# RWKV decay and a projections as three fp32r products on 64 rows each, masked scores in two buffers

## The reference, cut to what matters

```
r, rk, rv, wl, al = split(mixed, (512, 512, 512, 64, 64))     # mixed: (T, ...) after the token shift
w     = -softplus(-(w0 + tanh(wl) @ w_up)) - 0.5              # w_up: 64 x 512
decay = exp(-exp(w))
a     = sigmoid(a0 + al @ a_up)                               # a_up: 64 x 512
...                                                           # kk, rk, then the delta-rule scan
y     = rwkv7_scan(r, decay, rk, rv, kk, a)
```

## Time and profile before

| | |
|---|---|
| three runs | 3512.80, 3516.01, 3516.35 us, median 3516.01 |
| profiled execution | span 3515.1 us from its first to its last instruction; no time of its own is listed beside the span |
| PE | 3295.0 us busy, 94% of the span |
| DVE, ACT, POOL | 62%, 42%, 16% |
| granted TensorE clock, mean | 0.971 |
| the 32 projection matmuls, L274 | 64 records, from 40.2 to 817.4 us |

### The profile page before, as it was taken

The page is one execution under the profiler, slowest core; times in us unless marked ns, Lnnn a source line. Parts: engine busy times, 40 slices in busy tenths (PEclk is TensorE's granted clock), DMA queues, the critical chain, the costliest instruction groups (busy, mean ns, idle before and its releaser), DMA issues. The chain is left out here.

```text
span 3515.1 us, 75244 instructions
## 1 busy us (share of the span) xinstructions
PE 3295.0 (94%) x31246; PEld 2822.4 (80%) x31246; DVE 2186.4 (62%) x3701; ACT 1464.0 (42%) x2121; POOL 560.4 (16%) x792
## 2 busy tenths in 40 slices
PE   7999999999699998989979979949999999999997
PEld 5778888788577786867868868839999999999997
DVE  4666766667445655677777766666565655565563
ACT  5445444444255655332232223424444444444442
POOL 3455555554100000000000000000100110011000
PEclk9999999999899999989999999959999999999999
DMA  4221222211233434422121245436666666666662
GB/s 145 56 83 51 66 74 62 83 49 46 66 126 109 149 125 140 137 73 72 62 70 61 84 136 176 157 105 219 215 200 214 203 213 204 215 203 210 207 215 72
DMA packets 361838, 452.90 MB, mean 129 GB/s; under 512 B 15188, under 2 KB 300148, under 8 KB 361588
## 3 DMA queue, kind: packets, MB, share of 16 engines
q1 hardware_dynamic: 350200, 407.40, 35.7%
q0 software_dynamic: 9216, 33.56, 4.1%
q10 hardware_dynamic: 2176, 8.39, 0.6%
HBM read 382.17 MB, written 67.13 MB: 128 GB/s over the span
## 5 line engine op out<-in xcount | busy, mean ns | idle before, releaser
L2840 PE MATMUL bank<-ex_x_hi,ex_w_lo 128*128 128x256 f32 x2048 | 581.5, 284 | 2.0 <-DVE ex_x_lo L3022 2.0
L2841 PE MATMUL bank<-ex_x_lo,ex_w_hi 128*128 128x256 f32 x2048 | 580.2, 283 | 0.0
L2842 PE MATMUL bank<-ex_x_hi,ex_w_hi 128*128 128x256 f32 x2048 | 580.1, 283 | 0.0
L2836 DVE TENSOR_TENSOR ex_w_lo<-ex_w_loaded,ex_w_hi 128x2048 fp32r<-128x2048 f32 x192 | 433.9, 2289 | 226.7 <-ACT ex_w_hi L2832 222.3
L2832 ACT ACTIVATE ex_w_hi<-ex_w_loaded 128x2048 fp32r<-128x2048 f32 x192 | 359.4, 1904 | 172.5 <-PE bank L2842 169.3
L2840 PEld LDWEIGHTS bank<-ex_x_hi,ex_w_lo 128*128 128x128 f32 x2048 | 393.4, 192 | 2.8 <-issue 2.2
L2841 PEld LDWEIGHTS bank<-ex_x_lo,ex_w_hi 128*128 128x128 f32 x2048 | 393.5, 192 | 0.6
L2842 PEld LDWEIGHTS bank<-ex_x_hi,ex_w_hi 128*128 128x128 f32 x2048 | 393.5, 192 | 0.0
L2316 PE MATMUL bank<-sc_tokens_hi,sc_w_lo 128*128 128x512 f32 x672 | 267.7, 398 | 38.7 <-DVE hidden_hT_split L2428 16.0
L2896 POOL CAST ex_idx<-moe_idx_all 128x2 uint32 (+1 forms) x16 | 3.0, 186 | 1760.9 <-POOLq L79 1449.6
L2318 PE MATMUL bank<-sc_tokens_hi,sc_w_hi 128*128 128x512 f32 x672 | 265.0, 394 | 0.0
(11 more groups left out here) (485 smaller groups left out, 8312.5 us busy)
## 6 DMA issues: line engine op xcount, KB each, us to landing
ex_w_loaded<-in_wg SPq DMA_DIRECT2D x64, 1024.0 KB, 5.5
ex_w_loaded<-in_wu SPq DMA_DIRECT2D x64, 1024.0 KB, 6.5
ex_w_loaded<-in_wd SPq DMA_DIRECT2D x64, 1024.0 KB, 5.0
plain_weights<-in_w_in SPq DMA_DIRECT2D x70, 512.0 KB, 4.6
gl_ada_tile<-in_ada_w SPq DMA_DIRECT2D x48, 512.0 KB, 4.3
hidden_first_w<-in_sc_w_in SPq DMA_DIRECT2D x24, 1024.0 KB, 5.1
plain_columns<-hT_dram SPq DMA_DIRECT2D x14, 1024.0 KB, 7.4
plain_columns<-in_x SPq DMA_DIRECT2D x16, 512.0 KB, 5.7
```

Of the source, the lines that this page charges most:

```text
L2836: nc.vector.tensor_tensor(w_lo[c % SPLIT][:], raw[:, c % LOADED, :], w_hi[c % SPLIT][:].bitcast(F32), ALU.subtract).then_inc(s["lo"], 1)
L2840: nc.tensor.matmul(psum, ll, rh, start=first, stop=False)
L2841: nc.tensor.matmul(psum, lh, rl, start=False, stop=False)
L2842: return nc.tensor.matmul(psum, lh, rh, start=False, stop=last)
```

## The change

The projections become three fp32r products each, on the same 64 rows, in the order lo x hi, hi x lo, hi x hi, and in each of the three steps first the decay's matmul, then a's; both PSUM banks are taken ahead of the first. The operands `lup_hi`, `lup_lo` (once) and `lora_hi`, `lora_lo` (once a quarter) are made by ACT copies and DVE subtractions. The low parts lie where the plain `lup` and `lora` lay; the room for the high parts comes from the third `scm` buffer. PE now waits for `lora_lo`, and `low_lora` stands on DVE's list ahead of `mix_raw(i, "k", kx)`.

```
+        with Phase("rw_plain") as plain:
+            lup = sb(nc, plain, "lora_up", [P, HP, P])
+            lora = sb(nc, plain, "lora", [P, QT])
+        lup_lo = sb(nc, ctx, "lora_up_lo", [P, HP, P], F32R)
+        lora_lo = sb(nc, ctx, "lora_lo", [P, QT], F32R)
+        lup_hi = sb(nc, ctx, "lora_up_hi", [P, HP, P], F32R)
+        lora_hi = sb(nc, ctx, "lora_hi", [P, QT], F32R)
...
-        scm = [sb(nc, ctx, f"scores{i}", [P, 4, 4, 64]) for i in range(3)]
+        scm = [sb(nc, ctx, f"scores{i}", [P, 4, 4, 64]) for i in range(2)]
...
                 def decay_and_a(i):
-                    pe.wait_ge(s["lora"], i // HP + 1)
-                    for n in range(2):
-                        psum = begin(("wa"[n], i))
-                        nc.tensor.matmul(psum, lup[64 * n:64 * n + 64, i % HP, :], lora[64 * n:64 * n + 64, :], start=True, stop=True).then_inc(s["job"], 1)
+                    if i == 0:
+                        pe.wait_ge(s["up_lo"], 1)
+                    pe.wait_ge(s["lora_lo"], i // HP + 1)
+                    psums = [begin((name, i)) for name in "wa"]
+                    for m, (up, down) in enumerate(((lup_lo, lora_hi), (lup_hi, lora_lo), (lup_hi, lora_hi))):
+                        for rows, psum in zip(heads2, psums):
+                            mm = nc.tensor.matmul(psum, up[rows, i % HP, :], down[rows, :], start=(m == 0), stop=(m == 2))
+                            if m == 2:
+                                mm.then_inc(s["job"], 1)
...
                 def keep_lora(q):                                  # ACT
                     act.wait_ge(s["lmix"], q + 1)
-                    nc.scalar.activation(lora[0:64, :], lora[0:64, :], ACT.Tanh).then_inc(s["lora"], 1)
+                    nc.scalar.activation(lora_hi[64:128, :], lora[64:128, :], ACT.Copy)
+                    nc.scalar.activation(lora[0:64, :], lora[0:64, :], ACT.Tanh).then_inc(s["tanh"], 1)
+                    act.wait_ge(s["tanh"], q + 1)
+                    nc.scalar.activation(lora_hi[0:64, :], lora[0:64, :], ACT.Copy).then_inc(s["lora"], 1)
...
                 act.wait_ge(s["small"], 16 * SMALL)
+                nc.scalar.activation(lup_hi[:], lup[:], ACT.Copy).then_inc(s["up_hi"], 1)
...
+                def low_lora(q):                                   # DVE
+                    go.settle()
+                    dve.wait_ge(s["lora"], q + 1)
+                    nc.vector.tensor_tensor(lora_lo[:], lora[:], lora_hi[:].bitcast(F32), ALU.subtract).then_inc(s["lora_lo"], 1)
...
                         if (half, part) == (0, 2):
+                            low_lora(i // HP)
                             mix_raw(i, "k", kx)
...
+                dve.wait_ge(s["up_hi"], 1)
+                nc.vector.tensor_tensor(lup_lo[:], lup[:], lup_hi[:].bitcast(F32), ALU.subtract).then_inc(s["up_lo"], 1)
```

More of the change, by code:

```diff
@@ L117, in rwkv @@
             "hs0", "hs1", "hs2", "hs3", "w0", "w1", "w2", "w_hi", "w_lo", "job",
-            "lraw", "lmix", "lora", "tw", "sw", "ta", "cs", "pcs", "exps", "r_exp", "raw", "mixed", "kk", "kk_sq", "ssq",
+            "lraw", "lmix", "tanh", "lora", "lora_lo", "up_hi", "up_lo", "tw", "sw", "ta", "cs", "pcs", "exps", "r_exp", "raw", "mixed", "kk", "kk_sq", "ssq",
             "k_forms", "r_form", "rk", "n2_part", "n2", "tg", "gate", "bonus", "pre",
@@ L125, in rwkv @@
         wraw, w_lo, w_hi = [[whole[:, i * D:(i + 1) * D].rearrange("p (kb n) -> p kb n", n=P) for i in range(3)] for whole in (cols_buf.w, cols_buf.w_lo, cols_buf.w_hi)]
+        with Phase("rw_plain") as plain:
[5 more added lines that the diff above has]
+        lora_hi = sb(nc, ctx, "lora_hi", [P, QT], F32R)
         xst = sb(nc, ctx, "x_stat", [P, 4, 4])
         wc = sb(nc, ctx, "norm_cols", [P, KD])
-        lup = sb(nc, ctx, "lora_up", [P, HP, P])
         par = sb(nc, ctx, "head_params", [P, HP, 12])
@@ L133, in rwkv @@
         lraw = ob
-        lora = sb(nc, ctx, "lora", [P, QT])
         carry = sb(nc, ctx, "carry", [P, 2, HP, 3])
@@ L394, in inputs_of @@
                         for cr in heads2:
-                            mm = nc.tensor.matmul(bank[6][cr, p * C:p * C + C], scm[b % 3][cr, p, 2, :], tm[b % 3][cr, jj, 3, heads2[h]], start=True, stop=True)
+                            mm = nc.tensor.matmul(bank[6][cr, p * C:p * C + C], scm[b % 2][cr, p, 2, :], tm[b % 3][cr, jj, 3, heads2[h]], start=True, stop=True)
                     mm.then_inc(s["x"], 1)
@@ L415, in transfer @@
                             p, hs_, cr = 2 * h + jj, heads2[h], heads2[c]
-                            nc.tensor.matmul(bank[1 + c][hs_, 256 + jj * C:256 + jj * C + C], wun[cr, p, 0, :], scm[b % 3][cr, p, 1, :], start=True, stop=True)
+                            nc.tensor.matmul(bank[1 + c][hs_, 256 + jj * C:256 + jj * C + C], wun[cr, p, 0, :], scm[b % 2][cr, p, 1, :], start=True, stop=True)
                         for h, c in quads:
@@ L436, in y_inside @@
                         for cr in heads2:
-                            nc.tensor.matmul(bank[7][cr, o:o + C], scm[b % 3][cr, p, 3, :], tm[b % 3][cr, jj, 3, heads2[h]],
+                            nc.tensor.matmul(bank[7][cr, o:o + C], scm[b % 2][cr, p, 3, :], tm[b % 3][cr, jj, 3, heads2[h]],
                                              start=(p == 0), stop=False, skip_group_check=True)
                         for cr in heads2:
-                            mm = nc.tensor.matmul(bank[7][cr, o:o + C], scm[b % 3][cr, p, 1, :], wun[cr, p, 1, :],
+                            mm = nc.tensor.matmul(bank[7][cr, o:o + C], scm[b % 2][cr, p, 1, :], wun[cr, p, 1, :],
                                                   start=False, stop=False, skip_group_check=True)
@@ L1020, in keep_scores @@
                     for h in range(2):
-                        dst = scm[f % 3][:, 2 * h:2 * h + 2, :, :].rearrange("p j n t -> p j (n t)")
+                        dst = scm[f % 2][:, 2 * h:2 * h + 2, :, :].rearrange("p j n t -> p j (n t)")
                         nc.vector.tensor_tensor(dst, bank[1 + h].rearrange("p (j x) -> p j x", j=2), mk("scores").unsqueeze(1).to_broadcast([P, 2, 256]),
@@ L1159, in level_of @@
                     m = lm[:, l + 1, :].unsqueeze(1).to_broadcast([P, 2, C])
-                    nc.gpsimd.tensor_tensor(nt[:, l, 0:2, :], scm[g % 3][:, 0:2, 0, :], m, ALU.mult)
+                    nc.gpsimd.tensor_tensor(nt[:, l, 0:2, :], scm[g % 2][:, 0:2, 0, :], m, ALU.mult)
                     nc.gpsimd.tensor_tensor(nt[:, l, 2:4, :], across[:], m, ALU.mult).then_inc(s["nt"], 1)
@@ L1166, in corner @@
                     pool.wait_ge(s["n2"], i + 1)
-                    nil = scm[f % 3][:, :, 0, :]
+                    nil = scm[f % 2][:, :, 0, :]
                     by_head = nil.rearrange("p (h j) t -> p h j t", h=2)
@@ L1174, in corner @@
                     for c in range(2):
-                        ins = nc.gpsimd.tensor_copy(across[heads2[1 - c], :, :], scm[f % 3][heads2[c], 2:4, 0, :])
+                        ins = nc.gpsimd.tensor_copy(across[heads2[1 - c], :, :], scm[f % 2][heads2[c], 2:4, 0, :])
                     ins.then_inc(s["nil_across"], 1)
```

## The result

The changed kernel takes 3526.34 us (median of five runs, 3525.2 to 3535.2) against 3516.01 for the kernel before (3512.8 to 3518.31): ratio 1.0035, 95% interval 1.0025 to 1.0046. It is slower by 10.3 us, where no change was forecast; the time lies 0.34 us above the range. The profiled execution has a span of 3524.6 us and a mean granted clock of 0.971, as before.

The account below looks back on a forecast made before the run. PE, busy 94% of 3515.1 us, was taken to bound the kernel through its list. Terms of -2.1, +2.0 and 0 summed to -0.1 us, said as 3516.0 us, no change that can be told; range 3512.5 to 3526.

Parts of the forecast that it names:

- Side by side, 0.87 us: Projections on PE: both halves' fp32r matmuls overlap, three steps taking 0.87 us a tile against 1.06 for the plain ones.
- The twelve tiles: Tiles with `i % 4` not 0: 0.19 us less in eight, 0.14 in four held by DVE's L1043; 2.1 us less.
- Tiles 4, 8, 12, +0.68 each: `low_lora` ahead of `mix_raw(k)` delays `kx` and ACT's list behind it by 0.68 us each; 2.0 us more in all.
- Tile 0, start-up, score buffers, nothing: Added work hides behind existing waits in tile 0 and start-up; two score buffers bring no wait, no gain: 0 us.
- A: Projections: fp32r matmuls on different row halves run one after another; 9.6 us more, 3525.6 us; chance 0.19.
- B: Projections: each step pays its weight load, 0.32 us, so the twelve tiles gain about 0; +2.0, 3518 us; chance 0.05.
- D: Faster: the twelve tiles would have to gain 0.6 us each, which only new places in memory could do; chance 0.03.
- C: Clock falls to 1.2 GHz after PE's 1.9 us idle in tiles 4, 8, 12; 3 x 1.7 = +5.1, 3521 us; chance 0.05.

Follow-up runs that it names:

- the swapped order: The changed kernel with `mix_raw(k)` ahead of `low_lora` on DVE's list, PE's list as long as before: 3526.3 us, ratio 1.0028.
- the version without gaps: The changed kernel with 192 instructions of met waits added to PE's list, 128 at its head, 64 behind the first transposes: 3520.5 us, ratio 1.0012.
- the shift by 128: The changed kernel with 256 met waits, 128 instructions, at the head of PE's list: 3528.36 us, ratio 1.0045.

## Why the prediction was wrong

*Side by side, 0.87 us:* right. It measured 0.89 to 0.91, 0.16 less than the 1.06 of before instead of 0.19; in tiles 5, 9, 13 and 14 it is 1.02, 0.04 less instead of 0.14, and PE waits for L1063 there, as said. The 0.04 for 0.14 is a term of the sum that was mis-sized: from DVE's end to PE's start 0.05 us were taken, and 0.15 measured. The twelve tiles gave about 8 x 0.16 + 4 x 0.04 = 1.4 us, not 2.1.

*Tiles 4, 8, 12, +0.68 each:* the mechanism was right to the wait. `low_lora` took 0.68, PE idled 1.85, and the three slots lost 0.60 or 0.61 each: +1.8, not +2.0.

*Tile 0, start-up, score buffers, nothing:* nothing speaks against it beyond the spread of the start, 0.71 early to 1.46 late at the first `rw_E`; the two buffers alone measure 1.0005 with 1 inside the interval. That the two ACT operations are covered holds only with `low_lora` ahead of `mix_raw`, as the swapped order showed.

*Rivals:* A's serial matmuls, B's 0.32 steps and D are out by tile 6's rows. A would have given 3525.6, so the time that came lies where A put it, for another reason: without the pairs' rows one would have taken A for proven. C is not out. The mean granted clock is 0.971 in both, but the mean hides it: the stretch at 0.50 from 678.74 us comes behind tile 12's wait, as C has it, once in three times and for 0.9 us instead of 1.7. With the waits of 2.42 us of the swapped order it comes all three times and costs 1.0 to 1.6; in the version without gaps, with waits of 1.86 to 2.02, it does not come. What decides is not known.

*The step that failed* is the sum itself: "PE's list sets the time there, so a projection is worth what it takes on that list, plus or minus the waits around it". The list has another cost, its fetch. With 64 records more the boundaries of the 16 KB blocks moved by 4 a tile, out of stretches in which a crossing lasts over 5 us (so in the kernel before at five of the six places, and 3.34 us at 23490), into runs of 64-row matmuls, in which the 256 instructions are done in 2.5 to 3.9. In the profiled execution the six gaps cost 7.7 us and the lower clock behind one of them 1.6; the 0.9 behind tile 12's wait are C's. The forecast's own terms sum to -1.4 + 1.8 = +0.4 by their measured sizes, and the version without gaps shows +0.3 up to the third slot from the end and -1.1 up to the end of RWKV. So without the fetch the change would be worth nothing that can be told; that is worked out, since no version ran that shifts the list and pays nothing at its start.

One section of the Trainium skill speaks of this: "Runtime: NRT & Kernel Launch", Instruction fetch mechanics, says that instructions come in blocks of 16 KiB (256) over a DMA queue of the engine's own and that crossing a block is mostly hidden. The block size and the queue agree with the 188 packets of queue 8 and the period of 256. "Mostly hidden" holds for most of the crossings, but not for the six in 64-row matmuls here, which cost 7.7 us.

Open: what starts a fetch, and why it differs between executions of one kernel. In most gaps the packet starts 0.9 to 1.3 us behind the boundary. In others it starts later, up to 4.15 us under data and up to 5.40 with little of it (the gap of 2.02 us of the shift by 128); and in some executions it starts early enough for the gap to be missing. And no version that beats the kernel before was found: the best of the changed ones, 3520.5, still starts RWKV 2.0 us late.

## What to carry to other kernels

When an edit changes the number of instructions on a dense engine, look for idle time whose releaser is "issue" and for its distance in records before anything is read into a time of a few tenths of a per cent: a kernel with 48 instructions of met waits at its head differed as much as this change did. A control for such an edit is the old kernel with the same number of met waits, put where the engine idles longer than they take. And ask for the granted clock stretch by stretch: two stretches at half of it, 2.5 us of time, left the mean at 0.971.

## What the runs showed of the hardware

- In RWKV a crossing from one block boundary to the next, with the packet of a fetch inside it, took PE 3.08 us at the least in any run, and 3.16 to 7.93 where it had a gap. Crossings with no packet inside took from 2.32.
- PE resumes 1.1 to 1.6 us after the end of the 16 KB packet, in every gap at a block boundary of RWKV in every run.
- From 60 to 880 us the granted clock fell to 0.50 (1.2 GHz) only at idle times of PE of 0.76 to 3.15 us, with and without a releaser, and cost 0.9 to 1.6 us each time that it was worked out. It did not fall at each of them: at 2.02 us in tile 12 of the version without gaps it stayed at 1.00.
- fp32r matmuls on rows 0 to 63 and 64 to 127 run at the same time, 0.23 us a pair of 64x512 at the full clock, also when the list has three of one half ahead of three of the other.
- `nop` on PE left nothing in the program; a met wait did, two to an instruction, and each such instruction took PE 0.108 us (192 of them from 0.99 to 21.48 us). 64 of them behind the transposes made 2.3 us more of idle time there than in the changed kernel.
